# One change in four places of a two-block transformer kernel: squares, gate weights, an early score, and the last projection by halves of its rows

## The chip, the cores and the metric

The kernel runs on one core of a Trainium2 chip. The metric is the device time of one launch in microseconds, lower is better. The core has TensorE (PE, with a queue of its own for loading weights, PEld), VectorE (DVE), ScalarE (ACT), GpSimd (POOL) and SyncE (SP), which here only issues the loads of the weight stream.

## The reference

All values are fp32, 256 rows (positions) of width 1024. Two blocks follow each other, each two layers deep.

```
first block, per layer:
  h = rms_norm(x);  x += rms_norm(parallel_mixer(h) )      # RG-LRU, forgetting attention (8 heads), retention (4 heads)
  h = rms_norm(x);  x += rms_norm(cross_attention(h, mem)) # 4 heads, keys and values from 256 memory rows
  h = rms_norm(x);  x += rms_norm((silu(h Wg) * (h Wu)) Wd)
second block, per layer:
  h = rms_norm(x);  x += 0.5 * swiglu(h)
  h = rms_norm(x);  proj = h @ w_in      # queries, keys, values, 24 small gates, 3 x 1024 branch gates
  y_nsa = sparse attention, 8 heads: softmax over 15 compressed keys, over selected blocks (all of them at
          256 rows) and over a window, each weighted by sigmoid(small gate)
  y_sb  = stick-breaking attention, 4 heads;  y_swa = window attention with sinks, 4 heads
  merged = sum over branches of sigmoid(branch gate) * (y_branch @ w_up_branch)
  x += merged @ w_out
  h = rms_norm(x);  x += 0.5 * swiglu(h)
RG-LRU: a = exp(-8 r softplus(-lambda)), u = sqrt(1 - a^2) * (i * conv(x)), h = scan(a, u), times gelu(ly)
```

## The kernel before, in words

Everything is kept feature major: a tensor of 1024 features by 256 rows is 8 tiles of 128 features (partitions) by 256 rows, and tiles are handled in four pairs. Weights come as one stream in the order of use (ORDER, lines 51 to 56). A slot is 1024 x 256 weights, loaded in two halves of 512 KB into a ring of four buffers (line 2039). To keep fp32 accuracy, ScalarE writes the fp32r high half of each (w_hi, line 837), VectorE the rest (w_lo, line 1351), and TensorE makes three products, hi by hi, hi by lo and lo by hi (line 286). A slot is 48 products of 256 columns. `ahead(name)` in the programs of ScalarE and VectorE splits the slot that follows the one named; SP loads into a buffer again once its low half is made. So the order in which each engine works is written out by hand, one program per engine, and the engines meet at semaphores (a Signal's `at(n)` is waited for, its `next()` is sent).

**Norms.** A norm's scale is not applied to the input of a product but to its output. A slot that is fed (`fed=`, line 310) takes the input pair by pair as VectorE finishes its low halves (line 1373). ScalarE squares x (line 848), GpSimd adds the four pairs of squares into one (line 1964), and after the fed slot TensorE multiplies that one pair by a matrix of 1/1024 (lines 335 and 338), from which ScalarE takes the root (line 869) and VectorE the reciprocal (line 1389). In the first block the residual add before it is two multiplications and an add per pair (lines 1409 and 1413).

**First block's mixer.** After the slots rv, ck0, ck1, ck2 come two matrices of rotated features (line 439), the scores of the first two forget-attention heads (line 451), ck3, and then a loop in which TensorE turns (line 363) and multiplies (lines 358, 359) what ScalarE (exponentials, lines 1008 and 1009, copies, line 1016) and VectorE (maxima, line 1600, normalisation, line 1466) made of each head, with slot cv0 inside it. Beside ck0 to ck3 the RG-LRU runs: ScalarE's lambda operations (lines 984 to 992), VectorE's scaling of them (lines 1553 to 1559), its recurrence and the gelu product (lines 1562 to 1576), and the rotations (lines 1585 to 1588).

**Second block's mixer.** The last projections before the branch gates are v1 and sv. Between them TensorE runs 18 filler products (line 294, `keep_busy`), and the 24 small gates with x as the loaded operand and the gate weights moving (line 652, 24 columns). After sv come two heads of stick scores (line 676), then a loop over the eight sparse heads (scores at lines 696 to 700, maxima at line 1798, six exponentials at line 1232) with one slot of branch gates bg0 to bg11 beside each. up0 to up3 project the branches; VectorE multiplies with the sigmoids and adds (lines 1919 to 1924), and makes the merged pair's low half (line 1361). 24 fillers follow, and wo0 to wo3, each with all 1024 rows of w_out and 256 of its columns; wo0's second half waits for merged pair 3. Each slot gives one pair of output, added to x by VectorE (line 1932).

## Time and profile before

| | |
|---|---|
| median of 3 runs | 2326.41 us (2322.05 to 2326.66) |
| the profiled execution | 2324.44 us, span in the profile 2323.1 us |
| busy share: PE, DVE, ACT, POOL | 95%, 61%, 49%, 4% |
| mean granted TensorE clock | 0.973 of 2.4 GHz |
| moved from memory | 356.61 MB, 155 GB/s over the span |

PE's share counts any time in which a product is under way, fillers included, and says nothing of the clock at which it runs. The stages of the second block repeat in its two layers, those of the first in its two.

### The profile page before, as it was taken

What the parts mean: (1) busy time and instruction counts of PE and PEld (TensorE: products, weight loads), DVE (VectorE), ACT (ScalarE), POOL (GpSimd) and SP (SyncE); (2) the same over time, 40 slices, a digit from 0 to 9 for tenths busy, and PEclk for the clock granted to TensorE, in tenths of its full rate; (3) what the DMA queues carried; (4) which work ended last, traced back from release to release, by engine and by line L of the source; (5) the groups of instructions that cost most, each with busy time, mean ns of one, the idle gap of its engine ahead of it and who ended that gap; (6) DMA issues with size and microseconds to landing.
All of it is one profiled execution on the core that took longest, in us unless ns stands there. A gap on an engine that the chain in (4) does not pass through costs nothing.

```text
span 2323.1 us, 41302 instructions
## 1 busy us (share of the span) xinstructions
PE 2197.7 (95%) x17598; PEld 2104.4 (91%) x17598; DVE 1419.0 (61%) x2152; ACT 1131.7 (49%) x1758; POOL 91.0 (4%) x95
## 2 busy tenths in 40 slices
PE   6989899999889999999999999999999999999999
PEld 6868789999768899989998888999999998889999
DVE  5654665556547566566667567655666574667664
ACT  4554444434545444444546556444444455555443
POOL 4100000000000000000000000000000000000000
PEclk9989999999979999999999899999999988999999
DMA  5423246645324345646555224555566552234654
GB/s 208 151 85 128 83 148 205 211 145 177 114 73 134 108 160 186 199 156 197 190 195 175 81 91 131 171 187 189 176 197 204 179 171 91 91 122 151 195 192 159
DMA packets 98487, 360.36 MB, mean 155 GB/s; under 512 B 11136, under 2 KB 11149, under 8 KB 97920
## 3 DMA queue, kind: packets, MB, share of 16 engines
q1 hardware_dynamic: 96192, 349.22, 45.7%
q0 software_dynamic: 1680, 5.35, 0.7%
q8 instruction: 139, 2.28, 0.4%
q10 hardware_dynamic: 432, 3.15, 0.3%
q14 instruction: 44, 0.36, 0.0%
HBM read 356.61 MB, written 3.43 MB: 155 GB/s over the span
## 4 chain that ended last, share of the span: by engine, by line
PE 77%; DVE 14%; ACT 6%; issue 2%; DMA 0%; POOL 0%; DVEq 0%; ACTq 0%; SPq 0%; POOLq 0%
PE bank L286 68%; DVE w_lo L1351 4%; ACT w_hi L837 2%; PE bank L358 1%; DVE x L1413 1%; DVE xn_lo L1373 1%; DVE sq L1409 1%; PE bank L696 1%; PE bank L363 1%; DVE sq L1919 1%; PE bank L359 1%; DVE rinv L1731 1%; PE bank L354 0%; DMA raw<-in_stream 0%; DVE rinv L1403 0%
## 5 line engine op out<-in xcount | busy, mean ns | idle before, releaser
L1351 DVE TENSOR_TENSOR w_lo<-raw,w_hi 128x1024 fp32r<-128x1024 f32 x664 | 797.3, 1236 | 425.1 <-ACT w_hi L837 424.7
L286 PE MATMUL bank<-xn_hi,w_hi 128*128 128x256 f32 x3168 | 897.3, 283 | 53.4 <-DVE xn_lo L1373 43.2
L286 PE MATMUL bank<-xn_lo,w_hi 128*128 128x256 f32 x3168 | 887.4, 280 | 0.0
L286 PE MATMUL bank<-xn_hi,w_lo 128*128 128x256 f32 x3168 | 887.2, 280 | 0.0
L837 ACT ACTIVATE w_hi<-raw 128x1024 fp32r<-128x1024 f32 x664 | 673.6, 1051 | 255.1 <-PE bank L286 243.6
L286 PEld LDWEIGHTS bank<-xn_hi,w_hi 128*128 128x128 f32 x3168 | 602.4, 190 | 64.8 <-issue 51.0
L286 PEld LDWEIGHTS bank<-xn_hi,w_lo 128*128 128x128 f32 x3168 | 602.4, 190 | 0.0
L286 PEld LDWEIGHTS bank<-xn_lo,w_hi 128*128 128x128 f32 x3168 | 600.4, 190 | 1.1 <-issue 1.0
L286 PE MATMUL bank<-hid_hi,w_lo 128*128 128x256 f32 x1056 | 294.1, 279 | 0.0
L286 PE MATMUL bank<-hid_hi,w_hi 128*128 128x256 f32 x1056 | 294.1, 278 | 0.0
L286 PE MATMUL bank<-hid_lo,w_hi 128*128 128x256 f32 x1056 | 294.1, 278 | 0.0
L286 PEld LDWEIGHTS bank<-hid_hi,w_lo 128*128 128x128 f32 x1056 | 199.7, 189 | 0.0
L286 PEld LDWEIGHTS bank<-hid_hi,w_hi 128*128 128x128 f32 x1056 | 199.0, 188 | 0.0
L286 PEld LDWEIGHTS bank<-hid_lo,w_hi 128*128 128x128 f32 x1056 | 198.2, 188 | 0.0
L893 ACT ACTIVATE hid_hi<-act_t 128x512 fp32r<-128x512 f32 x66 | 41.8, 634 | 193.0 <-DVE act_t L1427 193.0
L889 ACT ACTIVATE act_t<-act_t 128x512 f32<-128x512 f32 x66 | 41.9, 635 | 184.9 <-DVE act_t L1422 184.9
L286 PE MATMUL bank<-y_hi,w_hi 128*128 128x256 f32 x384 | 107.3, 279 | 5.4 <-DVE y_lo L1361 4.6
L286 PE MATMUL bank<-y_hi,w_lo 128*128 128x256 f32 x384 | 106.4, 277 | 0.0
L286 PE MATMUL bank<-y_lo,w_hi 128*128 128x256 f32 x384 | 106.4, 277 | 0.0
L1964 POOL TENSOR_TENSOR sq<-sq 128x512 f32<-128x512 f32 x39 | 54.4, 1394 | 1319.0 <-ACT sq L848 1318.1
L286 PEld LDWEIGHTS bank<-y_hi,w_hi 128*128 128x128 f32 x384 | 72.1, 188 | 7.5 <-DVE y_lo L1361 3.6
L1361 DVE TENSOR_TENSOR hid_lo<-act_t,hid_hi 128x512 fp32r<-128x512 f32 x66 | 45.8, 693 | 50.8 <-ACT hid_hi L893 50.8
(351 smaller groups left out, 2854.6 us busy)
## 6 DMA issues: line engine op xcount, KB each, us to landing
raw<-in_stream SPq DMA_DIRECT2D x664, 512.0 KB, 4.2
skew<-vec POOLq DMA_DIRECT2D x12, 192.0 KB, 3.9
table<-skew POOLq DMA_DIRECT2D x1, 1408.0 KB, 7.3
con<-in_con ACTq DMA_DIRECT2D x1, 1029.0 KB, 14.9
x<-in_x ACTq DMA_DIRECT2D x1, 1024.0 KB, 6.8
xn<-in_mem ACTq DMA_DIRECT2D x1, 1024.0 KB, 11.5
out<-x SPq DMA_DIRECT2D x4, 256.0 KB, 3.3
logit<-in_small POOLq DMA_DIRECT2D x3, 288.5 KB, 3.0
```

The source lines that it names most:

```text
L286: m = T.matmul(out, a, b, start=first and j == 0, stop=True, skip_group_check=True)
L358: T.matmul(out, v_of(0), pT[:, 0:S], start=first, stop=False, skip_group_check=True)
L359: return T.matmul(out[:, P:S], v_of(1), pT[:, S:S + P], start=False, stop=last, skip_group_check=True)
L363: m = T.transpose(dst[:, to * P:(to + 1) * P], src[:, frm:frm + P], c("ident"))
L696: T.matmul(out[:, LATE], q[:, P:S], k, start=True, stop=True)
L837: AC.activation(w_hi[m % RING], raw[m % RING], ACT.Copy).then_inc(*hi_done.next())
L889: AC.activation(act_t, act_t, ACT.Silu).then_inc(*silu_made.next())
L893: AC.activation(hid_hi[:, 2 * j:2 * j + 2, :], act_t, ACT.Copy).then_inc(*hid_hi_made.next())
L1351: V.tensor_tensor(w_lo[m % RING], raw[m % RING], w_hi[m % RING].bitcast(F32), ALU.subtract).then_inc(*lo_done.next())
L1361: V.tensor_tensor(lo, src, hi.bitcast(F32), ALU.subtract).then_inc(*to.next())
L1373: m = V.scalar_tensor_tensor(xn_lo[:, k, :], x[:, k, :], gain[:, k:k + 1], xn_hi[:, k, :].bitcast(F32), ALU.mult, ALU.subtract)
L1964: G.tensor_tensor(sq[:, 0:2, :], sq[:, 0:2, :], sq[:, pair_of(b), :], ALU.add).then_inc(*summed.next())
```

## The change

It has four parts. First, for five norms (`by_pairs`: the cross attention's and the feed-forward's of both layers of the first block, and the second block's first) GpSimd no longer adds squares; TensorE multiplies all eight tiles of squares by the 1/1024 matrix, two after each pair of the fed slot. Second, in the first block ScalarE's lambda operations move to the forget gates, VectorE's scaling ahead of the convolution, the halves of slots ck3 and cv0 ahead of the gelu product's halves and of the softmax loop, and the rotations into that loop. Third, in the second block the fillers between v1 and sv go, the small gates are made with their weights loaded (24 columns) and x moving, then copied and turned back; the first stick scores stand ahead of sv and the first sparse head's scores between its two halves. Fourth, the last projection goes by halves of its rows: wo0 and wo1 hold the upper 512 rows of all columns, wo2 and wo3 the lower, into other banks; its fillers go.

```diff
+    gates_T = act_t[0:24, 0, :]
+    wo_out = [misc[0], misc[1], dense[1], acc[0]]
+    def wo_end(l, b):
+        return half_used.at(2 * SLOT_AT[("b2", l, "wo2")] + b + 1)
+    by_pairs = [norm_no(L, k) for L in range(DEPTH) for k in (1, 2)] + [norm_no(DEPTH, 0)]
...
+        def pair_of_squares(n, b):
+            T.wait_ge(*squared.at(4 * n + b + 1))
+            for k in (2 * b, 2 * b + 1):
+                m = T.matmul(misc[0][:, 0, :], avg, sq[:, k, :], start=k == 0, stop=k == KT - 1, skip_group_check=True)
+            if b == 3:
+                m.then_inc(*mean_made.next())
...
+                        if k == HK - 1:
+                            m.then_inc(*half_used.next())
+                        if k % 2 and squares is not None:
+                            pair_of_squares(squares, 2 * half + k // 2)
...
+                if n == 2:
+                    T.wait_ge(*rot_made.at(2 * L + 2))
                 if n >= 2:
                     fox_values(n - 2)
-            T.wait_ge(*rot_made.at(2 * L + 2))
...
-            keep_busy(18, mix_rows.at(3 * l + 1), dense[1])
             T.wait_ge(*wg_ready.at(l + 1))
-            T.wait_ge(*head_root.at(5 * l + 5))
+            T.wait_ge(*head_root.at(5 * l + 4))
-            for rt in range(2):
-                for k in range(KT):
-                    m = T.matmul(bank[4][:, rt * 24:(rt + 1) * 24], x[:, k, rt * P:(rt + 1) * P], wg[:, k, :],
-                                 start=k == 0, stop=k == KT - 1)
+            for k in range(KT):
+                m = T.matmul(bank[5][0:24, 0:S], wg[:, k, :], x[:, k, :], start=k == 0, stop=k == KT - 1)
             m.then_inc(*gate_made.next())
             cmp_turn(1)
-            project(9, slot_rows)
-            cmp_out_of(1)
...
             stick_scores(0)
-            stick_scores(1)
+            T.wait_ge(*gate_copied.at(l + 1))
+            for rt in range(2):
+                m = T.transpose(bank[5][:, S + rt * 24:S + (rt + 1) * 24], gates_T[:, rt * P:(rt + 1) * P],
+                                c("ident")[0:24, 0:24])
+            m.then_inc(*gate_turned.next())
...
+            project(9, slot_rows, between=lambda: nsa_scores(0))
+            cmp_out_of(1)
+            stick_scores(1)
             slot = 0
-            for n in range(8 + 2):
+            for n in range(1, 8 + 2):
...
-            keep_busy(24, None, misc[1])
-            T.wait_ge(*merged.at(4 * l + 3))
-            for b in range(4):
-                slot_T(at(f"wo{b}"), acc[b], merged_in_hi, merged_in_lo, second=merged.at(4 * l + 4) if b == 0 else None)
+            for i in range(4):
+                T.wait_ge(*(merged.at(4 * l + 2), branch_read.at(4 * l + 3), merged.at(4 * l + 4), merged.at(4 * l + 4))[i])
+                for part, r in halves(at(f"wo{i}")):
+                    b, half = 2 * (i % 2) + part, i // 2
+                    for ct in range(2):
+                        for k in range(HK):
+                            m = products(wo_out[b][:, ct, :], tile(r, k, slice(ct * P, (ct + 1) * P)),
+                                         [t[:, half * HK + k, :] for t in (merged_in_hi, merged_in_lo)], half == k == ct == 0)
+                    m.then_inc(*half_used.next())
```

ScalarE, first block:

```diff
             AC.activation(f8[:, 1, :], f8[:, 0, :], ACT.Abs, bias=small[0:8, SM1["fox_b"]]).then_inc(*f_abs.next())
+            AC.activation(stat[:, 0, 0:2], small_1("lam"), ACT.Abs).then_inc(*own.next())
...
+            AC.activation(stat[:, 0, 0:2], stat[:, 0, 0:2], ACT.Exp, scale=-1.0).then_inc(*own.next())
...
+            AC.activation(stat[:, 0, 0:2], stat[:, 0, 0:2], ACT.Ln, bias=one).then_inc(*lam_ln.next())
...
+            memory_slot(2)
             AC.wait_ge(*lru_made.at(L + 1))
             AC.activation(y_hi[:, 0:2, :], lru_h, ACT.Copy).then_inc(*lru_hi.next())
-            memory_slot(2)
+            memory_slot(3)
```

ScalarE, second block:

```diff
+            AC.activation(gates_T, bank[5][0:24, 0:S], ACT.Copy).then_inc(*gate_copied.next())
             cmp_turn(1)
             ahead(at("sv"))
-            out_rows(9, "sv")
-            cmp_out_of(1)
-            AC.wait_ge(*gate_made.at(l + 1))
+            AC.wait_ge(*gate_turned.at(l + 1))
...
             stick_exp(0)
-            stick_exp(1)
...
+            nsa_exps(0)
+            out_rows(9, "sv")
+            cmp_out_of(1)
+            stick_exp(1)
...
+            ahead(at("wo1"))
+            ahead(at("wo2"))
+            beside(0)
+            ahead(at("wo3"))
+            beside(1)
+            beside(2)
```

VectorE, first block:

```diff
             V.scalar_tensor_tensor(lru_u, lru_u, 1.0, lru_t, ALU.add, ALU.mult).then_inc(*root_in.next())
+            ahead(at("ck1"))
...
             V.wait_ge(*lru_made.last())
+            ahead(at("ck2"))
             low_half(y_lo[:, 0:2, :], lru_h, y_hi[:, 0:2, :], lru_hi.at(L + 1), own)
-            ahead(at("ck2"))
+            ahead(at("ck3"))
...
             for n in range(8 + 2):
                 if n < 8:
                     fox_softmax(n)
+                if n < 2:
+                    rotary(n)
+                if n == 2:
+                    ahead(at("cv0"))
```

VectorE, second block:

```diff
+                if b == 3:
+                    ahead(at("wo0"))
                 V.wait_ge(*branch_read.last())
...
             def add(b):
-                V.wait_ge(*slot_end(at(f"wo{b}")))
-                V.tensor_tensor(x[:, pair_of(b), :], x[:, pair_of(b), :], acc[b], ALU.add).then_inc(*x_updated.next())
+                V.wait_ge(*wo_end(l, b))
+                V.tensor_tensor(x[:, pair_of(b), :], x[:, pair_of(b), :], wo_out[b], ALU.add).then_inc(*x_updated.next())
```

GpSimd:

```diff
-                add_squares(norm_no(L, k))
+                if norm_no(L, k) not in by_pairs:
+                    add_squares(norm_no(L, k))
```

## Rows read from the trace of the kernel before

**Rows 1.** The page: busy time of each engine, and shares of the chain that ended last
```profile
PE 2197.7 (95%) x17598; PEld 2104.4 (91%) x17598; DVE 1419.0 (61%) x2152; ACT 1131.7 (49%) x1758; POOL 91.0 (4%) x95
PE 77%; DVE 14%; ACT 6%; issue 2%; DMA 0%; POOL 0%; DVEq 0%; ACTq 0%; SPq 0%; POOLq 0%
```
**Rows 2.** PE's waits, whole span: us in total, times, longest us
```profile
PE bank L286 <- DVE xn_lo L1373: 43.2, 19, 16.6
PE bank L286 <- DVE w_lo L1351: 22.0, 20, 3.0
...
PE bank L286 <- DVE merged_lo L1361: 6.4, 2, 3.3
```
**Rows 3.** Windows: stretch, length, busy us and count per engine, clock; steady, low clock
```profile
900.00:1000.00 100.00, 100.00 (x851) 100.00 (x850) 54.04 (x52) 43.26 (x48) 0.00 (x0) 1.00 0.59 191
1905.00:1915.00 10.00, 10.00 (x50) 10.00 (x48) 6.13 (x4) 1.62 (x2) 0.00 (x0) 0.50 0.39 136
```
**Rows 4.** Windows of the five joins: the first, and the sum of all five
```profile
236.30:248.30 12.00, 8.45 (x53) 8.04 (x53) 10.26 (x14) 5.36 (x10) 4.02 (x3) 0.86 0.08 25
...
sum 53.40, PE 35.72 PEld 33.65 DVE 48.26 ACT 26.77 POOL 20.13; mean PE 7.14 PEld 6.73 DVE 9.65 ACT 5.35 POOL 4.03
```
**Rows 5.** Timeline of the fourth join, DVE, then POOL: start, duration, instruction
```profile
811.04 0.69 DVE L1413 TENSOR_TENSOR x<-x,sq 128x512 f32<-128x512 f32 x1
811.65 0.87 DVE L1373 SCALAR_TENSOR_TENSOR xn_lo<-x,small,xn_hi 128x256 fp32r<-128x256 f32 x2
...
813.34 1.76 DVE L1413 TENSOR_TENSOR x<-x,sq 128x512 f32<-128x512 f32 x1
...
813.29 1.27 POOL L1964 TENSOR_TENSOR sq<-sq 128x512 f32<-128x512 f32 x1 [7.95 <-ACT sq L848]
```
**Rows 6.** Groups of PE in the fourth join: busy us, mean ns
```profile
L335 PE MATMUL bank<-sq,avg 128*128 128x256 f32 x4 | 1.0, 378 | 0.0
```
**Rows 7.** Windows, first block, end of ck1 to end of cv0, both layers
```profile
121.20:160.90 39.70, 32.36 (x181) 27.25 (x180) 26.19 (x63) 20.46 (x41) 0.00 (x0) 0.79 0.30 94
617.90:657.90 40.00, 30.39 (x186) 25.31 (x187) 26.19 (x63) 20.98 (x41) 0.00 (x0) 0.83 0.27 90
```
**Rows 8.** PE's waits from 609 to 658 us, second layer of the first block
```profile
PE bank L286 <- DVE w_lo L1351: 5.1, 2, 3.0
...
PE bank L363 <- DVE logit L1466: 3.5, 3, 1.8
```
**Rows 9.** Timeline there: a table load of ACT, two low halves of DVE
```profile
611.02 1.28 ACT L986 ACT_TABLE_LOAD   x1
...
618.62 2.36 DVE L1351 TENSOR_TENSOR w_lo<-raw,w_hi 128x1024 fp32r<-128x1024 f32 x2 [3.95 <-ACT w_hi L837]
```
**Rows 10.** Windows, second block, end of v1 to end of bg0, both layers
```profile
1273.30:1306.90 33.60, 30.25 (x196) 28.25 (x195) 12.11 (x46) 18.75 (x47) 0.00 (x0) 0.80 0.24 79
1931.20:1965.40 34.20, 31.17 (x197) 28.94 (x195) 11.70 (x46) 18.43 (x47) 0.00 (x0) 0.75 0.23 78
```
**Rows 11.** Groups of PE from 1273.3 to 1306.9 us: busy, mean ns, idle before
```profile
L652 PE MATMUL bank<-small,x 128*128 128x24 f32 x32 | 5.3, 326 | 0.5 <-ACT root L1118 0.5
...
L696 PE MATMUL bank<-proj 64*128 64x256 f32 x8 | 3.8, 561 | 2.8 <-DVE stat L1798 1.6 <-ACT stat L1208 1.2
...
L294 PE MATMUL bank<-ones 128*128 128x256 bf16 x18 | 2.1, 272 | 0.0
```
**Rows 12.** DVE's wait for six exponentials, 1273 to 1308 us
```profile
DVE stat L1807 <- ACT logit L1232: 2.6, 1, 2.6
```
**Rows 13.** Windows, end of the up slots to end of the next gate slot, both layers
```profile
1449.50:1485.70 36.20, 32.93 (x267) 32.38 (x267) 24.19 (x30) 17.93 (x26) 4.60 (x4) 0.95 0.48 154
2108.20:2143.30 35.10, 32.02 (x268) 31.54 (x267) 22.66 (x30) 17.80 (x26) 4.25 (x3) 0.95 0.46 150
```
**Rows 14.** From 1449 to 1487 us: a wait of PE, an instruction of DVE
```profile
PE bank L286 <- DVE merged_lo L1361: 3.3, 1, 3.3
...
1482.14 1.92 DVE L1373 SCALAR_TENSOR_TENSOR xn_lo<-x,small,xn_hi 128x256 fp32r<-128x256 f32 x2 [0.98 <-ACT xn_hi L856]
```

More of the change, by code:

```diff
@@ L303, in halves, with slot_T @@
                 yield half, m % RING
-        def slot_T(name, out, hi, lo, cts=(0, 1), fed=None, second=None):
+        def pair_of_squares(n, b):
[4 more added lines that the diff above has]
+                m.then_inc(*mean_made.next())
+        def slot_T(name, out, hi, lo, cts=(0, 1), fed=None, second=None, squares=None):
             for half, r in halves(name):
@@ L321, in slot_T, with slot_rows @@
                                          [t[:, half * HK + k, :] for t in (hi, lo)], half == 0 and k == 0 and ct == cts[0])
-                m.then_inc(*half_used.next())
-        def slot_rows(name, out, hi, lo):
+                    m.then_inc(*half_used.next())
+        def slot_rows(name, out, hi, lo, between=None):
             for half, r in halves(name):
+                if half and between:
+                    between()
                 for rt in range(ST):
@@ L366, in ffn @@
         def ffn(f, fed, n):
-            slot_T((f, "gate", 0), dense[0], xn_hi, xn_lo, fed=fed)
-            norm_scale(n)
+            slot_T((f, "gate", 0), dense[0], xn_hi, xn_lo, fed=fed, squares=n if n in by_pairs else None)
+            if n not in by_pairs:
+                norm_scale(n)
             for j in range(FB):
@@ L1534, in vector_program @@
             ahead(at("rv"))
+            st = lambda n: stat[:, n, 0:2]
+            V.wait_ge(*lam_ln.at(L + 1))
+            V.tensor_scalar(st(1), small_1("lam"), -1.0, 0.0, ALU.mult, ALU.max).then_inc(*own.next())
+            V.wait_ge(*own.last())
+            V.tensor_tensor(st(1), st(1), st(0), ALU.add).then_inc(*own.next())
+            V.wait_ge(*own.last())
+            V.tensor_scalar(st(2), st(1), -8.0, None, ALU.mult)
+            V.tensor_scalar(st(3), st(1), 8.0, None, ALU.mult).then_inc(*lam_scaled.next())
             lx = proj[:, 7, :, :]
@@ L2113, in dense, with dense_by_halves @@
             put(pair(w[:, c:c + COLS]))
+    def dense_by_halves(w):
+        blocks = [pair(w[:, c:c + COLS]) for c in range(0, w.shape[1], COLS)]
+        for half in range(2):
+            rows = [b[:, half * SLOT // 2:(half + 1) * SLOT // 2] for b in blocks]
+            put(np.concatenate(rows[0:2], 1))
+            put(np.concatenate(rows[2:4], 1))
     def ffn(gate, up, down):
```

100 lines of the change are left out of this document (45 added, 55 removed).

## The prediction

> **What bounds the kernel now.** I read the page's busy shares and its chain first: TensorE is busy 95% of the span and carries 77% of the chain that ended last, VectorE 14% [rows 1]. So a stage is worth what TensorE loses in it, in three forms: waits, products at the lower clock, and filler. The list of TensorE's waits names the places [rows 2]: it waits 43.2 us for the low halves of the normed input, 22.0 us for the low halves of weights and 6.4 us for the merged branches. A steady stretch gives the price of a product: 100 us hold 851, 0.1175 us each, 5.64 us for a slot of 48; in another stretch at granted clock 0.50, the 1.2 GHz level, 10 us hold 50, 0.20 us each, so a slot costs about 4 us more there [rows 3]. The rest is read stage by stage.
>
> **Part 1: squares added on TensorE at five joins.** From the first product of the fed slot until the mean is under way, the five joins take 53.4 us together, the first 12.0, the others about 10.35, with TensorE busy 35.7 in all [rows 4]. While GpSimd adds squares, VectorE's residual add takes 1.76 us instead of 0.69 [rows 5], twice a join; without GpSimd each shrinks by 1.07, and pairs of tiles come every 2.3 us (0.87 + 0.87 + 0.69, less overlap) instead of 3.4. That would be 2.1 us a join. But the change gives TensorE eight fp32 products where two stood. Two of them, recorded as four, took 1.0 us with the tail of the last [rows 6]; without it I put one at 0.43, so eight cost 3.4. A pair now holds 12 products and 0.86 of squares, 2.3 us: TensorE becomes the bound as VectorE lets go. The join is then 5.64 + 3.44 + 0.2 of semaphores = 9.3, a gain of 1.0 in each of four and of 2.3 in the first, where the clock had dropped to a mean of 0.86: 6 us. Bounds: 4, if squares arrive late, and 9, if TensorE finds a pair of squares free in waits that remain. The root, table load and reciprocal behind the mean stay where they were.
>
> **Part 2: the lambda chain and the rotations in the first block.** The stage from the end of slot ck1 to the end of cv0 takes 39.7 and 40.0 us in the two layers; TensorE idles 7.3 and 9.6 in it, and the mean clock of 0.79 and 0.83 says that over a third of it runs at 1.2 GHz [rows 7]. In the second layer 5.1 us of the idle time are two waits for the low halves of ck2 and ck3 and 3.5 are softmax waits [rows 8]. The first wait is made by ScalarE, which loads tables of 1.28 us between tiny lambda operations [rows 9]; two such loads and three tiny operations, about 3.3 us, leave this chain. They share the Exp and Ln tables of the forget gates, where they add only about 0.7 us of ScalarE work. VectorE now makes ck3's low halves (2.36 us a slot [rows 9]) before the GeLU product's low half, and puts the rotations, six 0.69 us operations, behind the first softmax. So softmax 0 starts before ck3 ends, not after it. I take the 5.1 us and the first softmax wait, 1.8 us [rows 8], as gone: 6.9. Late next are the rotations: TensorE's first values wait until both are made, in the place of softmax 1's wait, so I credit nothing more. Against it: the lambda work now stands before the convolution on VectorE (four tiny operations, 0.65 us, in front of a waiting TensorE in the first layer) and in front of the forget gates' scan (0.35 us in the second). 6.5 net, twice 13; bounds 4.5 (softmax wait back) and 9.5 (cv0 entirely at full clock) a layer. The slots keep their order on SP's queue; their loads wait for low halves, which come earlier.
>
> **Part 3: branch gates with their weights loaded, first scores inside the sv slot.** From v1's end to bg0's end: 33.6 and 34.2 us, mean clock 0.80 and 0.75 [rows 10]. It holds 18 fillers (2.1 us), 32 records of gate products that take 5.3 us [rows 11] and the scores of heads 0 and 1 with 2.8 us of waits [rows 11]. With weights loaded, the gates are eight products of 256 columns, 8 x 0.43 = 3.4 us [rows 6]. The new order costs: norms 0.6, gates 3.4, turns and transposes 0.7, one stick head 0.9, half of sv 2.8, scores 2.0, the other half 2.8, the v output 0.6, a wait 1.8, stick head 0.9, scores 2.0, bg0 5.6: 24.1. The wait is new: the second stick head needs the sv rows read by ScalarE, which now does head 0's six exponentials before; VectorE waited 2.6 us for such six [rows 12]. The Sigmoid's table load stands beside sv's first half. So 9.5 and 10.1 us if the clock stays full. The stage still has narrow products (24 and 15 columns), so I take off one short low stretch, 1.3 us a layer: 17 us for both. Bounds: 10 (as low as before) and 20. Behind bg0 everything keeps its distance, since the loop there is TensorE's own.
>
> **Part 4: last projection by halves of its rows.** Before: 36.2 and 35.1 us from the end of the up slots to the end of the next gate slot [rows 13]. In it are 24 fillers (2.8 us at the price of the 18 in [rows 11]), a wait of 3.3 us for merged pair 3 [rows 14] and a short low-clock stretch (mean 0.95 [rows 13]). Now pairs 0 and 1 suffice to begin; only wo0's low halves are waited for, 0.7 us. wo1 finds its low halves, made right after the last branch products; merged pair 3 is ready some 10 us in, before wo2 needs it at 12. So 0.7 + 192 x 0.1175 = 23.3. What becomes late is the tail: outputs 0 to 3 are whole only in the last 11 us, so the adds, high halves, squares and low halves of four pairs bunch up behind VectorE, and GpSimd still adds squares here; its presence stretches a pair of low halves from 0.87 to 1.92 [rows 5, 14]. Pair 2 comes about 3 us after the slot starts, pair 3 about 5.5 to 7; the gate slot takes 7.4 to 9.1 instead of 5.7. Sum 30.7 to 32.4: gains 3.8 to 5.5 and 2.7 to 4.4; 8 us for both. Bounds 3 and 11.
>
> **Sum.** 6 + 13 + 17 + 8 = 44 us off the profiled execution's 2324.44: 2280.4. The median of the runs shown is 2.0 above it, 2326.41, so against that 2282. I give 2281.
>
> **A rule against the change.** The filler rows stand where TensorE would idle [rows 11], and low-clock stretches follow idle or narrow work [rows 7, 10]. The Trainium skill, "TensorE: Matmul & The Clock Gate", section "Why this matters for your kernels", says to keep TensorE continuously busy, since idle gaps between bursts put it back to half rate; dropping 18 and 24 fillers a layer goes against it. By that page alone parts 3 and 4 would keep or enlarge their low stretches; by the rows the fillers did not prevent any, as every one of these stages had one [rows 10, 13].
>
> **Rivals.**
> A, the clock takes its share: low stretches stay as long as they were in parts 2 and 3, and one of 17 us like that in the steady part of the second layer's mix appears once more. Part 2 gives 4.5 a layer, part 3 gives 10 in all, one such stretch costs up to 7: 6 + 9 + 10 + 8 - 7 = 26, so 2299. For it: mean clocks of 0.75 to 0.83 with fillers in place. Against: the waits around which they lie shrink.
> B, the stretches vanish with the waits: 9 + 19 + 20 + 11 = 59, so 2266. Against: GpSimd's contention in part 4 and the rotation wait stay.
> C, slower: without filler TensorE sits at 1.2 GHz through the branch-gate loop of both layers, from sv to the up slots. A slot there costs 4 us more [rows 3]; the 44 us are used up when 11 slots more than now run low; if half of the 24 bg and 8 up slots did, 16, it would cost 64 us and give 2345. Against: this loop has full slots with hardly a wait between.
> D, the joins bring nothing and part 4's tail eats its head (squares or low halves arrive after TensorE asks): 13 + 17 = 30, so 2296.
>
> **Chances.** Forecast (2270 to 2292) 0.65, A 0.13, B 0.09, C 0.02, D 0.09; 0.02 that parts 2 and 3 move nothing because another engine's chain sets them. Range 2266 to 2297: it takes in B's and D's ends and leaves A's worst and C out. A measurement here can tell about 0.2%, 4.6 us, from no change; faster by more 0.96, within 0.02, slower 0.02.
>
> **What the changed profile would show.** Part 1: GpSimd's adds gone from five joins, residual adds at 0.69 us, joins near 9.3 with TensorE busy almost throughout. Part 2: no wait of L286 for low halves at ck2 and ck3; a wait for the rotations instead. Part 3: v1's end to bg0's end near 24 us, the gate group at some 3.5 us for 16 records a layer, a wait of about 1.8 before the second stick head. Part 4: no wait for merged pair 3, new waits for xn_lo in the gate slot. I am wrong if the granted clock is lower over whole slots, if ScalarE's high halves become what sv or bg0 waits for, or if the tail's low halves cost more than 4 us.

## The result, and the profile after

| | before | changed |
|---|---|---|
| median, first comparison | 2324.23 us (2320.61 to 2326.66, 4 runs) | 2261.62 us (2260.1 to 2266.29, 4 runs) |
| ratio | | 0.9739, 95% interval 0.9699 to 0.9778 |
| the profiled execution | 2324.44 us, span 2323.1 us | 2260.1 us, span 2258.8 us |
| busy share: PE, DVE, ACT, POOL | 95%, 61%, 49%, 4% | 96%, 62%, 50%, 3% |
| mean granted TensorE clock | 0.973 | 0.983 |

The change gives 62.6 us where I forecast 44, and 2261.6 lies 4.4 us under the low end of the range. The page of the changed kernel, busy time and chain, against [rows 1]:

```profile
PE 2163.3 (96%) x17546; PEld 2067.9 (92%) x17546; DVE 1404.4 (62%) x2152; ACT 1124.3 (50%) x1756; POOL 71.0 (3%) x80
...
PE 78%; DVE 13%; ACT 6%; issue 2%; DMA 0%; POOL 0%; ACTq 0%; DVEq 0%; SPq 0%; POOLq 0%
```

TensorE has 34 us less to do and waits for 30 us less. The 52 records that are gone cannot be 34 us; so its products themselves have become cheaper, by their clock or in some other way. I read the four parts first and then the rest.

**Part 1.** Windows of the five joins of the changed kernel, the first and the sum (columns: stretch; length; busy us and count of PE, PEld, DVE, ACT, POOL; granted clock; DMA share; GB/s), and VectorE's timeline in the fourth (start, duration, instruction):

```profile
233.74:243.14 9.40, 9.40 (x66) 8.81 (x67) 7.64 (x14) 5.28 (x10) 0.00 (x0) 1.00 0.10 29
...
sum 46.87, PE 46.87 PEld 43.73 DVE 38.17 ACT 26.38 POOL 0.00; mean PE 9.37 PEld 8.75 DVE 7.63 ACT 5.28 POOL 0.00
```
```profile
790.81 0.69 DVE L1458 TENSOR_TENSOR x<-x,sq 128x512 f32<-128x512 f32 x1
791.42 0.87 DVE L1418 SCALAR_TENSOR_TENSOR xn_lo<-x,small,xn_hi 128x256 fp32r<-128x256 f32 x2
...
793.12 0.69 DVE L1458 TENSOR_TENSOR x<-x,sq 128x512 f32<-128x512 f32 x1
```

TensorE is busy throughout, GpSimd is gone, and both residual adds take 0.69 us (one took 1.76 in [rows 5]). By these windows 53.4 us [rows 4] became 46.9, but those of the changed kernel end 0.4 us later, in the next slot. From the first product of the fed slot to the first of the next one, a join takes 9.0 us where 9.3 was forecast, and the five went from 52.9 to 45.1: 7.8, against 6. In all twelve profiles with this part each of the five takes 9.0 to 9.1 us; in the eight without it 10.2 to 10.3, or 11.8 to 11.9 with a short stretch at low clock.

**Part 2.** Windows of TensorE: the stage of [rows 7] (end of ck1 to end of cv0) after the change; then the longer stage from the forget gates' first products to the first retention mean, of the kernel before and of the changed one:

```profile
119.80:153.80 34.00, 29.26 (x188) 24.82 (x187) 21.76 (x59) 17.50 (x38) 0.00 (x0) 0.85 0.36 120
602.40:637.50 35.10, 30.50 (x187) 25.79 (x186) 22.06 (x59) 17.68 (x38) 0.00 (x0) 0.81 0.35 119
```
```profile
96.90:189.40 92.50, 79.69 (x485) 0.89 0.28 91
590.20:687.60 97.40, 81.52 (x484) 0.84 0.26 87
160.90:189.40 28.50, 23.08 (x139) 1.00 0.16 55
657.90:687.60 29.70, 24.25 (x133) 0.89 0.17 56
```
```profile
95.40:186.30 90.90, 80.17 (x485) 0.86 0.29 93
575.90:668.10 92.20, 81.36 (x484) 0.85 0.29 92
153.80:186.30 32.50, 27.10 (x133) 0.81 0.11 33
637.50:668.10 30.60, 25.16 (x133) 0.89 0.11 34
```

The forecast's own window gained 5.7 and 4.9 us (6.5 each forecast). But behind cv0 the rest of the stage, the last two rows of each fence, went from 28.5 and 29.7 to 32.5 and 30.6. In the first layer that is the clock, 1.00 before and 0.81 after: TensorE idles 5.4 us in both rows. The whole stage gained 1.6 and 5.2: 6.8 us, not 13. This pair of profiles shows less than most: in the mean of all eight profiles without the part the stage takes 93.2 and 95.6 us, of all nine with the change's order 88.4 and 91.5, a gain of 4.8 and 4.1, so 9. What became late is in TensorE's waits from 118 to 160 us (us in total, times, longest), and on VectorE's timeline:

```profile
PE bank L387 <- DVE logit L1511: 2.9, 2, 2.2
PE bank L382 <- DVE lru L1634: 1.4, 1, 1.4
PE bank L382 <- ACT probT L1057: 1.1, 1, 1.1
```
```profile
131.94 0.55 DVE L1511 TENSOR_SCALAR logit<-logit,stat 128x256 f32<-128x256 f32 x2
132.40 0.69 DVE L1631 TENSOR_TENSOR lru<-proj,cos 128x512 f32<-128x512 f32 x1
133.00 0.69 DVE L1632 TENSOR_TENSOR lru<-bank,sin 128x512 f32<-128x512 f32 x1
133.73 0.69 DVE L1634 TENSOR_TENSOR lru<-lru,lru 128x512 f32<-128x512 f32 x1
134.34 0.42 DVE L1646 CUSTOM_DVE_ANT_0 logit<-bank,xn 128x256 f32<-128x256 f32 x1
```

Softmax 0 is hidden by ck3, as planned. But the first rotation (132.40 to 134.4) now stands in front of softmax 1, and TensorE waits 2.2 us for that softmax (L1511), then 1.4 for the second rotation (L1634).

**Part 3.** Windows, end of v1 to end of bg0, both layers [rows 10]; below, from 1250 to 1274 us, TensorE's gate group and its one wait:

```profile
1250.50:1273.90 23.40, 22.00 (x163) 18.77 (x162) 11.86 (x46) 18.75 (x48) 0.00 (x0) 1.00 0.33 113
1879.60:1904.30 24.70, 23.30 (x163) 20.07 (x162) 13.16 (x47) 18.90 (x48) 0.00 (x0) 0.93 0.34 106
```
```profile
L675 PE MATMUL bank<-x,small 128*24 128x256 f32 x16 | 3.6, 380 | 0.0
```
```profile
PE bank L696 <- ACT proj L1199: 1.4, 1, 1.4
```

33.6 and 34.2 became 23.4 and 24.7, where 24.1 (25.4 with a short low stretch) was worked out: 19.7 us against 17. The small gates, which the prediction calls branch gates, take 3.6 us in 16 records (3.4 forecast), the new wait 1.4 (1.8), and the clock full in one layer.

**Part 4.** Windows, end of the up slots to end of the next gate slot [rows 13], and the wait from 1445 to 1456 us:

```profile
1416.50:1448.10 31.60, 28.89 (x242) 28.50 (x242) 23.68 (x30) 17.65 (x26) 4.60 (x4) 1.00 0.52 176
2048.60:2078.90 30.30, 28.86 (x241) 28.52 (x242) 22.37 (x30) 17.59 (x26) 4.39 (x3) 1.00 0.54 174
```
```profile
PE bank L296 <- DVE xn_lo L1418: 0.7, 1, 0.7
```

36.2 and 35.1 became 31.6 and 30.3 (30.7 to 32.4 forecast): 9.4 us against 8. The wait for merged pair 3 is gone, a wait for xn_lo stands in the gate slot.

**What is left.** The four parts make 7.8 + 6.8 + 19.7 + 9.4 = 43.7 us by their own stages, against 44 forecast, while the spans differ by 64.3. The other 20 us lie in code that the change does not touch. Windows of TensorE inside the first and fourth feed-forward and over the second layer's mix up to v1's end; first the kernel before, then the changed one (columns: stretch; length; busy us and count; clock; DMA share; GB/s):

```profile
350.00:450.00 100.00, 100.00 (x852) 1.00 0.63 205
1500.00:1600.00 100.00, 100.00 (x852) 1.00 0.58 186
...
1849.50:1931.80 82.30, 79.09 (x589) 0.90 0.45 149
```
```profile
350.00:450.00 100.00, 100.00 (x885) 1.00 0.68 219
1500.00:1600.00 100.00, 100.00 (x885) 1.00 0.61 195
...
1805.10:1880.00 74.90, 71.65 (x587) 1.00 0.50 166
```

TensorE is busy without a gap at clock 1.00 in both kernels, and yet has 885 products in 100 us in one and 852 in the other. From start to start they stand 113.3 or 117.8 ns apart (a window also counts two or three products that began before it). A feed-forward holds one of the two spacings from its third slot, where TensorE waits for low halves of weights and starts anew, to its end, 1488 products: 6.7 us. Of the six, three stood at 117.8 before and one after: 13.4 us. The low stretch in the mix is the other 7.4. 43.7 + 13.4 + 7.4 = 64.5, the 64.3 of the spans to within 0.2.

### The profile page after: what moved, and what is told of

Read it like the earlier page. It is cut to its first block, busy times and chain, and to the rows that moved or that the text cites. A ratio compares the mean times of both kernels' runs of the same rounds, so it can differ in the third digit from the quotient of the medians.

```text
span 2258.8 us, 41175 instructions
## 1 busy us (share of the span) xinstructions
PE 2163.3 (96%) x17546; PEld 2067.9 (92%) x17546; DVE 1404.4 (62%) x2152; ACT 1124.3 (50%) x1756; POOL 71.0 (3%) x80
## 4 chain that ended last, share of the span: by engine, by line
PE 78%; DVE 13%; ACT 6%; issue 2%; DMA 0%; POOL 0%; ACTq 0%; DVEq 0%; SPq 0%; POOLq 0%
PE bank L296 69%; DVE w_lo L1396 4%; ACT w_hi L875 2%; PE bank L382 2%; DVE rinv L1779 1%; PE bank L319 1%; PE bank L387 1%; PE bank L383 1%; PE bank L720 1%; DVE xn_lo L1418 1%; DVE x L1458 1%; DVE sq L1454 1%; DVE sq L1966 1%; PE bank L378 0%; DMA raw<-in_stream 0%
## 5 line engine op out<-in xcount | busy, mean ns | idle before, releaser
L1472 DVE TENSOR_TENSOR act_t<-act_t,bank 128x512 f32<-128x512 f32 x66 | 45.4, 687 | 46.4 <-PE bank L296 46.4
```

The costliest lines, as they stand in the source:

```text
L1472: V.tensor_tensor(act_t, act_t, dense[1], ALU.mult).then_inc(*up_read.next())
```

## The experiments

Times are medians with the range of their executions. In all comparisons together the kernel before ran 75 times, from 2302.7 to 2341.2 us, with medians of 2318 to 2324 in each. The theory: the parts are worth their stages, and the rest is spacing and stretches, which no part brings. The rival: some part does bring them.

**Each part alone, in the kernel before** (the core of each edit; the rest of the part as in the change's diff)

```diff
+    by_pairs = [norm_no(L, k) for L in range(DEPTH) for k in (1, 2)] + [norm_no(DEPTH, 0)]
```


> The kernel before with part 1 alone (squares of five joins added by TensorE). My theory: the part itself is worth what the two traces differ by at the five joins, 6 to 7 us, and it also changes how the feed-forward behind a join starts, so that the feed-forward of the first layer runs with its products 113 ns apart where they stood 118 ns apart before, some 7 us more: 2309 to 2312 in all. Rival: the joins alone, 2317, the spacing of the products being chance. Second rival: GpSimd's absence speeds other stages too, 2300.


```diff
+                if n < 2:
+                    rotary(n)
```


> The kernel before with part 2 alone (lambda chain among the forget gates, low halves of ck3 early, rotations behind the first softmaxes). My theory from the trace after: 7 us, because the rotations, 2 us each, now stand in front of softmax 1 and of the first values and give back what the earlier slot gains: 2317. Rival (the prediction's own term): 13 us, 2311, the rest of it having been lost after the change only to the clock. Second rival: 3 us or less, the remainder of the 7 having come from part 1's joins.


```diff
-            keep_busy(18, mix_rows.at(3 * l + 1), dense[1])
+            project(9, slot_rows, between=lambda: nsa_scores(0))
```


> The kernel before with part 3 alone (branch gates with their weights loaded, first scores inside the sv slot, 18 fillers gone). My theory: 18 us, 9 a layer, 2306. Rival: 26 us, 2298, if the 17 us stretch at the low clock in the second layer's mix, in code that the part does not touch, goes with the part and not by chance. Second rival: the fillers held the clock, so that without them the part gives under 10 us, 2314 or more.


```diff
-            keep_busy(24, None, misc[1])
+        dense_by_halves(a["w_out_2"][l])
```


> The kernel before with part 4 alone (last projection by halves of its rows, 24 fillers gone). My theory: 9 us from the part and 7 us more, since the feed-forward behind the first of the two projections ran with its products 118 ns apart and now starts anew at 113: 2308. Rival: the part alone, 2315. Second rival: the late adds eat it, 2320 or more.

Measured, against 2320.9 for the kernel before: part 1 2319.1 (2302.8 to 2335.5), ratio 0.9992, interval 0.9961 to 1.0024; part 2 2320.5 (2302.6 to 2329.8), 0.999, 0.9962 to 1.0018; part 3 2292.4 (2286.5 to 2315.2), 0.9895, 0.9845 to 0.9945; part 4 2306.0 (2293.1 to 2312.3), 0.9922, 0.9894 to 0.9949. So 2, 0, 29 and 15 us. As medians, none of the sizes expected for parts 1 to 3 came out, though the intervals are wide: part 2's holds the 7 us of its theory, part 3's both 18 and 26. Part 4's did, but not as it was put together: in its profile the feed-forward behind the first last projection did stand at 113 ns, while the one after it, at 113 before, stood at 118. By stage the parts were there in full: part 3's 43 us from the key mean to the first values were 32.3 in both layers. What hid them is the executions' own scatter of 19 to 33 us. In the five profiles up to here that are built on the kernel before, 13 of 30 feed-forwards stood at 113.3 ns, in a different pattern each time.

**The changed kernel again, and three edits of it.** The second waits for TensorE's own last product ahead of gate 1, the third puts fp32 products ahead of gate 2, the fourth puts the fillers back.

> The changed kernel as it is, to see how far one execution stands from the next. In the six profiles so far every one of the 36 feed-forwards starts anew at a wait in its third slot and then holds one spacing of products, 113.3 or 117.8 ns, to its end; 18 of the 36 took the fast one, in no order. My theory: that is drawn anew in each execution, each draw worth 1500 products x 4.5 ns = 6.8 us, so executions scatter by some 20 us around a mean that is the four parts, 41 to 44 us, under that of the kernel before: 2277 to 2282 on this chip if the kernel before has 2321, a ratio of 0.981 to 0.983. Rival: the spacing follows from the code, and the ratio is again 0.974.


```diff
+                    if j == 0:
+                        T.wait_ge(*slot_end((f, "up", 0)))
```


> The changed kernel, with TensorE waiting for its own last product of slot up 0 before gate 1 in each feed-forward, a pause of some 0.2 us. Theory that any restart draws anew: same mean as the changed kernel plus 6 x 0.2 = 1.2 us, fast and slow spacing in the profile both. Rival: a restart of this kind always comes out fast; then all six feed-forwards run at 113.3 ns and the mean is 3 x 6.8 = 20 us lower than that of the changed kernel, with a narrow scatter. Third: it always comes out slow, 20 us higher.


```diff
+                    if j == 1:
+                        for k in range(2):
+                            T.matmul(misc[1][:, 0, :], avg, sq[:, k, :], start=k == 0, stop=k == 1)
```


> The changed kernel, with two extra fp32 products of 256 columns (into an unused half of a bank) right before gate 2 in each feed-forward. Wherever products followed fp32 ones without a pause in the profiles so far, they ran 118 ns apart. Theory: all six feed-forwards run at 117.8 from there on, against three of six by chance: 3 x 6.5 = 19 us, and 6 x 1.0 us for the products themselves: 25 us above the changed kernel, with less scatter. Rival: the spacing is not touched by what stands ahead: 6 us above it.


```diff
+            keep_busy(18, mix_rows.at(3 * l + 1), dense[1])
...
+            keep_busy(24, None, misc[1])
```


> The changed kernel with the 18 and 24 fillers of the kernel before put back where they stood (ahead of the branch gates and ahead of the last projection), twice each. Theory: they hold no clock here, and where no wait is left to cover they are paid in full: 2 x (2.1 + 2.8) = 9.8 us less the 0.9 of wait at the last projection twice, 8 us slower than the changed kernel. Rival, the rule that TensorE is to be kept busy: the low stretches around them get shorter, and it is the same or up to 5 us faster.

The changed kernel again: 2267.2 (2253.6 to 2277.4, 6 runs), ratio 0.9741, interval 0.9705 to 0.9778. The ratio of the first comparison came back, so the surplus is no accident of four runs; my 0.981 to 0.983 fell. But the code does not fix the spacing either. Windows of this execution (2276.1 us), first and fourth feed-forward:

```profile
350.00:450.00 100.00, 100.00 (x851) 1.00 0.65 210
...
1500.00:1600.00 100.00, 100.00 (x851) 1.00 0.59 193
```

These are the same two that ran at 885 in the first profile of the same code. This execution had four of six at 117.8 ns where the other had one, and its span is 17.3 us longer. Three more slow feed-forwards make 20; it also has a stretch of 17 us at low clock in the second layer's mix, and less time at low clock in the first block (49 against 54 us in part 2's stages).

The wait for the last product, 2271.2 (2261.1 to 2279.9), told nothing: it stood ahead of the wait for low halves at the same place, which ends later. The fp32 products: 2302.2 (2294.9 to 2305.5), 35 us longer, with all six feed-forwards at 117.8 ns, two of which had run at 113 until the fp32 products came. One row, third feed-forward:

```profile
1050.00:1150.00 100.00, 100.00 (x852) 1.00 0.58 185
```

Products that follow fp32 ones without a pause took the long spacing at all six places. That is no rule for every fp32 product: most slots of branch gates, which start 0.2 us behind the last fp32 score product, stood at 113 in the same profile. The 25 us that I gave for it started from three of six; against all six at 113 (2256.5, below) it is 46 by the medians and 40 by the ratios to the kernel before of each comparison, where 6 x 6.5 + 6 x 1.0 = 45 would be due.

The fillers: 2280.4 (2273.5 to 2302.0), 13 us longer than the changed kernel beside it, 8 expected. The stage of part 3 in the first layer, to be set against 23.40 at clock 1.00 above:

```profile
1240.70:1269.00 28.30, 26.89 (x181) 23.07 (x180) 13.29 (x47) 18.70 (x48) 0.00 (x0) 0.88 0.29 98
```

18 fillers are 2.1 us; the other 2.8 are the clock, lower with the fillers than without. It is one execution, but none of the nine others of the changed kernel and its variants has any time at low clock in this stage of the first layer. In the second layer the fillers had 3.4 us of it, the others 0 to 7. So the rule weighed in the prediction brought nothing in this stage (the Trainium skill, "TensorE: Matmul & The Clock Gate", section "Why this matters for your kernels"): the fillers kept TensorE busy and the clock fell all the same. Nor is it the missing fillers that raised the clock. The kernel before has 7 to 20 us at low clock here, the changed one with the same fillers 7 and 3, so most of the gain comes with the new order and the wide gate products; which of the two was not tried.

**Six kinds of restart, and two orders of part 2**

```diff
+            if kind in (0, 3, 5):
+                T.wait_ge(*slot_end((f, "up", j)))
+            if kind == 1:
+                T.matmul(out, b16[:, 0:P], b16, start=True, stop=True)
+            if kind in (2, 3):
+                T.matmul(out[:, 0:64], b16[:, 0:P], b16[:, 0:64], start=True, stop=True)
+            if kind in (4, 5):
+                T.matmul(out[:, 0:P], xn_hi[:, 0, 0:P], xn_hi[:, 0, 0:P], start=True, stop=True)
```


> The changed kernel with ten restarts of one kind in each feed-forward, one ahead of each gate slot from the second on, another kind in each: in the first a wait for TensorE's own last product; in the second a bf16 product of 256 columns; in the third a bf16 product of 64 columns; in the fourth the wait and then that narrow one; in the fifth a product of 128 columns in the format of the others; in the sixth the wait and then that one. 60 draws in one profile. Theory that only a pause draws anew, evenly: first, fourth and sixth mixed (some 5 of 10 fast), second slow throughout as behind fillers. Rival: one kind gives the 113.3 ns spacing ten times of ten, and would be the way to make all feed-forwards fast, 3 x 6.8 = 20 us under the changed kernel's mean. The time itself is 60 x 0.1 to 0.2 us longer than the changed kernel's.

Windows of 10 us between restarts: three in the second feed-forward (one bf16 product of 256 columns each time), three in the fourth (the wait and a 64-column bf16 product):

```profile
833.00:843.00 10.00, 10.00 (x91) 1.00 0.59 179
844.00:854.00 10.00, 10.00 (x90) 1.00 0.58 172
855.00:865.00 10.00, 10.00 (x90) 1.00 0.56 184
...
1455.00:1465.00 10.00, 9.85 (x88) 1.00 0.72 224
1466.00:1476.00 10.00, 9.85 (x84) 1.00 0.55 172
1477.00:1487.00 10.00, 9.85 (x88) 1.00 0.52 172
```

This was one execution (2286.3 us). The first restart of each feed-forward stands ahead of the wait for low halves and tells nothing, so each kind has nine. No kind drew at random. After TensorE's own pause (first) and after one bf16 product without a pause (second) the spacing was 113 ns nine times of nine, but both kinds also found it there, so they may only keep it. The 64-column product without a pause (third) found 118 once, made it 113, and kept that eight times. With the pause and the narrow product (fourth), the 128-column product (fifth) and the pause with that one (sixth) it changed at every restart, 88, 84, 88 in the rows. So for the last three the spacing depends on the state in which the restart finds TensorE. That it comes out either way behind a wait for another engine because that engine's signal arrives at any moment is my reading, and was not tried by itself.

```diff
+            for n in range(2):
+                rotary(n)
...
-                if n < 2:
-                    rotary(n)
```


> The changed kernel with both rotations ahead of the first softmax on VectorE again, the rest of part 2 kept. Theory: moving the rotations behind the softmaxes gained nothing, since TensorE now waits 2.2 us for softmax 1 behind the first rotation and 1.4 us for the second one, where it would wait some 2.9 us for softmax 0: within 1 us a layer of the changed kernel, its waits between the end of ck3 and the first values the same 3 to 4 us. Rival (the prediction's step): the move was worth 1.8 us a layer, so this is 3.6 us slower.


```diff
-                if n in (1, 4):
-                    memory_slot(3 + n // 4)
+                if n in (1, 2):
+                    memory_slot(2 + n)
```


> The changed kernel with slot cv0 two steps earlier on TensorE (behind the third head's scores), its high halves right behind ck3's on ScalarE and its low halves between softmax 0 and the first rotation on VectorE. Theory: the 5.6 us of cv0 cover the waits for softmax 1 and the rotations (2.2 + 1.4 us), and what they covered before, a wait of 3 us for cv0's own low halves, goes too: 2.5 us a layer, 5 us in all below the changed kernel, in the trace at the same spacing and clock. Rival: VectorE's chain through the eight softmaxes and two rotations sets the end of the loop, and the waits turn up behind it: no gain.

Rotations first: 2249.2 (2246.0 to 2254.1), ratio 0.9689, interval 0.964 to 0.9738. cv0 early: 2251.1 (2246.1 to 2262.3), 0.9697, 0.9651 to 0.9744. Both lie 10 to 18 us under the changed kernel's two medians; the expectations were no gain for the first and 5 us for the second. But the stage of part 2 is not where they gain: from the forget gates to the retention mean it takes 88.4 and 91.0 us with the rotations first, 88.7 and 90.7 with cv0 early, and 88.6 and 91.6 in the mean of six profiles of the changed kernel with the change's order. So moving the rotations behind the softmaxes brought nothing, and early cv0 nothing in this run. Five of six feed-forwards stood at 113 in both profiles, and neither had the 17 us stretch in its mixes. Why they are shorter than the changed kernel is not shown.

**The spacing fixed.** From here each feed-forward has the third kind of restart ahead of gates 2 and 3:

```diff
+                    if j in (1, 2):
+                        T.matmul(misc[1][:, 0, 0:64], ones.bitcast(BF16)[:, 0:P], ones.bitcast(BF16)[:, 0:64], start=True, stop=True)
```


> The changed kernel with one bf16 product of 64 columns, without a pause, ahead of gate 2 and of gate 3 in each feed-forward. In the profile with six kinds of restart, that kind left the 113.3 ns spacing nine times of nine. Theory: all six feed-forwards run at 113.3 from there on in every execution, so the time is some 3 x 6.5 = 19 us under the changed kernel's mean of 2265, 2246, and the scatter shrinks to that of the clock stretches. Rival: the kind only keeps the spacing that it finds; then the six are mixed and the time is that of the changed kernel, 2262 to 2268.

> The kernel before with the same two narrow products in each feed-forward. Theory: all six feed-forwards at 113.3 ns, 2321 - 19 = 2302, and the distance to the changed kernel with the same products is what the four parts are worth without the spacing: by the stages of thirteen profiles 9 + 9 + 21 + 10 = 49 us, a ratio of 0.979. Rival: the distance stays at the measured 60 us, a ratio of 0.974, and the surplus over the parts was no matter of the feed-forwards' spacing.

> The variant with slot cv0 early, with the same two narrow products. Theory: its lead of some 15 us over the changed kernel came from its feed-forwards (five of six fast in its profile); with the spacing taken out it ends within 2 us of the changed kernel with the same products. Rival: early cv0 was worth it in the loop itself, and it stays 5 us or more ahead, the fastest of all.

In the changed kernel 2256.5 (2251.2 to 2262.2), in the kernel before 2294.7 (2293.7 to 2296.5), with early cv0 2252.0 (2246.0 to 2258.8); against 2318.4 for the kernel before as it is, ratios 0.9725 (0.9674 to 0.9775), 0.9894 (0.985 to 0.9937) and 0.971 (0.9666 to 0.9755). Fourth and first feed-forward of the kernel before with the narrow products:

```profile
360.00:460.00 100.00, 100.00 (x885) 1.00 0.69 216
...
1520.00:1620.00 100.00, 100.00 (x885) 1.00 0.61 198
```

Twelve products of 64 columns take 24 us off the kernel before and shrink its scatter from 34 us, in the same comparison, to 3. All six feed-forwards are at 113.3 ns, in this profile and in the six others with these products, 42 of 42; 21 of them ran at 117.8 until the first narrow product came, and none after it. The distance of the pair is 38 us, a ratio of 0.983 (0.980 to 0.986 between the extremes of the two), where it was 62.6 and 56.9 us, both times a ratio of 0.974 (0.970 to 0.978), with the spacing left free. So 19 to 24 us of the distance went when the spacing was fixed; my forecast lacks 18.6. How it divides is less sure. The kernel before lost 24 us by it in one and the same comparison. The changed kernel was not timed without the narrow products there: 2256.5 is 5 and 11 us under its medians in the two other comparisons, but the kernel before stood 6 us lower here than in both, so it may have lost anything from nothing to 11. The six runs of the changed kernel fall into 2251.2 to 2252.0 and 2261.1 to 2262.2, and the profiled one, of the upper three, has the stretch at low clock in the second layer's mix that the kernel before had in its first profile:

```profile
1167.20:1242.10 74.90, 71.68 (x589) 1.00 0.50 164
1796.40:1878.60 82.20, 79.21 (x589) 0.90 0.46 149
```

If the lower three runs are without it, which no profile shows, the parts are worth 43 there. Early cv0 is 4.5 us shorter than the changed kernel with the spacing fixed, 3.2 of them in the stage (87.4 and 88.6 us against 88.1 and 91.1). That lies between the two expectations, but the runs of the two overlap (2246.0 to 2258.8 and 2251.2 to 2262.2), so a lead is likely and not shown. It and the rotations first are the shortest measured, too close together to be ordered.

**Each part alone, the spacing fixed** (same edits as at the start, with the two narrow products)

> Part 1 alone in the kernel before, now with the two narrow products in each feed-forward, so that the spacing no longer covers what the part is worth; to be set against the kernel before with the same products, 2294.7. Theory, by the joins' own time in the traces: 8 to 9 us, 2286. Rival (the prediction's term): 6 us, 2289. Second rival: nothing, 2294, as its first timing seemed to say.

> Part 2 alone, with the narrow products, against 2294.7. Theory: 8.6 us, the mean difference of the stage from the forget gates' scan to the retention mean in the traces with and without the part, 2286. Rival (the prediction's term): 13 us, 2282.

> Part 3 alone, with the narrow products, against 2294.7. Theory: 9 us a layer by its stage against that kernel's own 42.0 and 40.6 us (32.3 with the part), 18 in all, 2277. Rival: 26 us, 2269, if the part also keeps the feed-forwards or the stretches in the mix from the slow side, as its first timing of 2292 against 2321 suggested.

> Part 4 alone, with the narrow products, against 2294.7. Theory: 5 us a layer by its stage (36.1 and 35.0 against 30.4), 10 in all, 2285. Rival (the prediction's term): 8 us, 2287. Second rival: 15 us, 2280, as its first timing of 2306 against 2321 suggested.

| | with the narrow products | less than 2294.7 | first timing gave | stages of the two first profiles | forecast |
|---|---|---|---|---|---|
| part 1 | 2291.8 (2289.6 to 2299.0) | 3.0 | 2 | 7.8 | 6 |
| part 2 | 2290.4 (2286.3 to 2298.5) | 4.3 | 0 | 6.8 | 13 |
| part 3 | 2275.0 (2270.9 to 2278.6) | 19.7 | 29 | 19.7 | 17 |
| part 4 | 2286.6 (2284.5 to 2289.3) | 8.1 | 15 | 9.4 | 8 |
| sum | | 35.1 | 46 | 43.7 | 44 |
| all four | 2256.5 (2251.2 to 2262.2) | 38.2 | 62.6 | | |

Within their uncertainty the parts add. These runs were on another chip than the pair; the kernel before as it is stood 2.5 us apart on the two (2318.4 and 2321.0), so each difference is sure to some 3 us, by my estimate. Set against the kernel before timed beside them, each part would be worth 2.5 us more: 5.5, 6.8, 22.2 and 10.7. That is enough to put part 2 far under 13, and not enough to choose between 3 and 7.8 for part 1. My own expectations for parts 1 and 2, 8 to 9 us from the stages in many profiles, are above what came; those for parts 3 and 4, 18 and 10, are within 2. The short low-clock stretches may take some of it back: in part 1's profile the first layer's mixer stage, which the part does not touch, took 95.2 us against 92.6 in the kernel before with the same narrow products, with 7 us more at low clock. That is one profile of each, and not shown beyond it.

## Why the prediction was right and wrong

**The step that failed** is the price of a product, put at one value from one stretch ("0.1175 us each, 5.64 us for a slot of 48"), and with it the silent assumption that feed-forwards which the change does not touch cost the same before and after. The kernel has two prices at full clock, 113.3 and 117.8 ns, and a feed-forward takes one or the other for 1488 products. With the spacing fixed in both kernels the distance is 38 us against 44 forecast; with it free the distance is 57 to 63. So the surplus goes with the spacing: 13.4 us in the two first profiles, with 7.4 of the low-clock stretch beside it. That 2261.6 lies below the range is the term that I left out. That the four stages sum to 43.7 against 44 is in part luck: part 2 gave 6 us less than its term, and the other three together 6 more. What is open is why the free spacing favours the changed kernel. Its time says so in both comparisons, but the counts hardly do: 13 of 30 feed-forwards short in the profiles built on the kernel before, 7 of 12 in the two of the changed kernel. My range took in bounds for each part and none for the code outside them, though the trace of before already had feed-forwards of both kinds side by side, 852 and 885 products in 100 us. And "about 0.2%, 4.6 us" for what a measurement can tell came from three runs; 75 of the same kernel spread over 38 us. A smaller slip is the price at low clock, 0.20 us from 50 products in 10 us: from start to start it is 0.213, so a slot costs 4.6 us more there, not 4.

**Part 1** was right by its own stage (7.8 against 6), with 9.0 us a join and the add at 0.69. The sum was low by its own numbers: five joins of 9.3 in place of [rows 4] make 6.9, since the first gains 2.7 and not 2.3. With the spacing fixed it brought 3.0 (5.5 by the kernel before beside it), one us under my lower bound, though within its uncertainty.

**Part 2** was mis-sized: 13 forecast, 6.8 by stage in the first pair (9 in the mean of all profiles), 4.3 to 6.8 by time. Its first half was right: the waits for low halves went and the forecast's window shrank by 5.7 and 4.9. The step "late next are the rotations ... in the place of softmax 1's wait" named the right wait, but took it as one for one. Rotation 0 delays softmax 1 by its 2 us, and rotation 1 comes on top. That the first softmax wait would be "gone" counted a wait as removed that had moved: with the rotations first again the stage takes the same time. What the stage gained in the mean, 4.8 and 4.1 us, is about the 5.1 us of waits for low halves without the 1.8 of that softmax. The 4 us that the first layer lost behind cv0 in the first pair are low clock.

**Part 3** was right in its mechanism and order, 23.4 and 24.7 us against 24.1 to 25.4, and slightly low as a term (19.7 against 17), since I held back for the clock. **Part 4** was right: 8.1 and 9.4 against 8, both stages at the edge of or inside 30.7 to 32.4.

**The rivals.** A was right for part 2 and wrong for part 3. Part 2's stage has as much time at low clock with the part (23 and 27 us in the mean) as without (22 and 25), and the gain is near A's 4.5 us a layer. In part 3's stage, where the fillers went, the clock rose. B's time, 2266, was nearly met for another reason: part of its gain was to be the stretches gone with the waits, and part 3's stage did reach full clock, but parts 2 and 4 did not give their upper bounds. C and D did not happen. The stretch of 17 us in the mix is a matter of chance as A had it, only with the other sign: it was there in the profile before and not in the one after; over all twenty profiles the changed kernel and its variants had it in 5 of 20 mixes, the kernel before and its variants in 5 of 20.

## What to carry to other kernels

Before pricing a change by stages, count products per 100 us in several unchanged stretches at full clock: if two spacings show, one execution is no baseline, and a stage that nobody touched can move more than the one that was changed. Fix what scatters (here twelve narrow products, themselves worth 1% to the kernel before) and then time the parts; at a scatter of some 35 us parts of 3 to 20 us were timed as 0 to 29. And a wait that is moved is not a wait removed: look for what the moved work now stands in front of.

## What the runs showed of the hardware that was not expected

Weight load and product pairs of 256 columns at full granted clock run 113.3 or 117.8 ns apart, each for hundreds of products on end. The Trainium skill, "TensorE: Matmul & The Clock Gate", section "Back-to-back issue gap", has a formula for an isolated product, by which an estimate for 256 columns is 109 ns, and says that in a stream the weight load has a share in the spacing, with figures for 128 and 512 columns. The 18 bf16 fillers [rows 11] stand 109 ns apart in the trace of before and agree with the formula; the stream of fp32r pairs stands 4 and 9 ns above it. The long spacing followed behind fp32 products at all six places of the run made for it, while 0.2 us behind the fp32 scores of the branch-gate loop it was mostly the short one; a single bf16 product of 64 columns in the middle of the stream ended in the short one, 42 of 42 feed-forwards, 21 of which had the long one until then. A restart after a wait for another engine gave either: 35 of 66 short, over eleven profiles without such products. Why a kernel leans to one side (17 of 30 long in the profiles built on the kernel before; five of six short in each of the two variants of part 2) stays open. So does what sets off the 17 us at low clock in the mix, where nothing that the profile shows differs between executions.
